# Turned weight blocks moved by sixteen transfers instead of ScalarE copies, with a new order of the last pair and a split last store

## The reference

```python
proj = h @ w_in[i]                      # token-mixer | memory query | gate columns
...
scores = jnp.einsum('bqhmd,bkhmd->bhmqk', q_blk, k) * scale
scores = jnp.where(causal, scores, NEG_BIG)
probs = jax.nn.softmax(scores, axis=-1)
weights = probs[:, :, 0] - lam * probs[:, :, 1]
out = jnp.einsum('bhqk,bkhe->bqhe', weights.astype(v.dtype), v)   # then RMSNorm per head
...
branch = jnp.concatenate([tok_out, cross_out], axis=-1) * jax.nn.silu(gate)
y = branch @ w_out[i]
x = x + _rms_norm(y, post_norm[i])
```

## Time and profile before

| | us |
|---|---|
| median of 3 runs (lowest to highest) | 956.06 (955.55 to 956.22) |
| the profiled execution | 956.12 |
| its span, first to last instruction | 954.3 |
| TensorE busy | 939.1 (98%) |
| VectorE busy | 632.1 (66%) |
| ScalarE busy | 504.3 (53%) |
| GpSimd busy | 1.2 |
| ScalarE's block copies, line 988, 96 in all | 34.6 |
| mean granted TensorE clock | 0.994 |

### The profile page before, as it was taken

How to read it: one execution, slowest core, us unless ns; L and a number is a source line. 1 busy time by engine, 2 the same in 40 slices (tenths; PEclk the granted TensorE clock), 3 DMA queues, 4 the chain that set the end, 5 groups by cost and what they waited for, 6 DMA issues and landing times.

```text
span 954.3 us, 12693 instructions
## 1 busy us (share of the span) xinstructions
PE 939.1 (98%) x4784; PEld 795.1 (83%) x4784; DVE 632.1 (66%) x826; ACT 504.3 (53%) x801; POOL 1.2 (0%) x9
## 2 busy tenths in 40 slices
PE   9999999999999999999999999999999999979996
PEld 7888888888888888888888888888888888868885
DVE  5878765754665475555685567466788888876555
ACT  6767633444434434444465456437577576574442
POOL 0000000000000000000000000000000000000000
PEclk9999999999999999999999999999999999989998
DMA  9757467667766666676566645664764764744552
GB/s 333 241 162 242 150 195 210 194 195 220 209 200 187 191 197 219 221 242 240 167 226 199 194 139 194 182 213 134 220 198 141 213 197 134 241 138 155 195 198 88
DMA packets 123870, 186.35 MB, mean 195 GB/s; under 512 B 6765, under 2 KB 66477, under 8 KB 123306
## 3 DMA queue, kind: packets, MB, share of 16 engines
q1 hardware_dynamic: 122138, 178.80, 60.2%
q10 hardware_dynamic: 1680, 6.85, 2.0%
HBM read 178.82 MB, written 2.10 MB: 190 GB/s over the span
## 4 chain that ended last, share of the span: by engine, by line
PE 96%; DVE 1%; DMA 1%; issue 1%; ACT 1%; SPq 0%; POOL 0%; DVEq 0%; POOLq 0%; ACTq 0%
PE psum L410 22%; PE psum L471 19%; PE psum L472 19%; PE psum L473 19%; PE psum L411 11%; PE psum L663 1%; DMA stage_area<-in_mem_dram 1%; PE psum L490 1%; PE psum L534 0%; DVE lo_ring L1040 0%; PE psum L511 0%; PE psum L652 0%; PE psum L644 0%; PE psum L643 0%; PE psum L642 0%
## 5 line engine op out<-in xcount | busy, mean ns | idle before, releaser
L1040 DVE TENSOR_TENSOR lo_ring<-raw_ring,hi_ring 128x1024 fp32r<-128x1024 f32 x318 | 386.0, 1222 | 261.7 <-ACT hi_ring L718 261.3
L718 ACT ACTIVATE hi_ring<-raw_ring 128x1024 fp32r<-128x1024 f32 x318 | 335.6, 1062 | 374.6 <-PE psum L473 275.3
L410 PE MATMUL psum<-hT_split,hi_ring 128*128 128x512 f32 x832 | 292.7, 397 | 0.0
L411 PE MATMUL psum<-hT_split,lo_ring 128*128 128x256 f32 x832 | 232.1, 279 | 0.0
L410 PEld LDWEIGHTS psum<-hT_split,hi_ring 128*128 128x128 f32 x832 | 156.1, 188 | 37.9 <-issue 2.0
L471 PE MATMUL psum<-hi_ring,hT_split 128*128 128x512 f32 x480 | 187.1, 390 | 0.0
L472 PE MATMUL psum<-lo_ring,hT_split 128*128 128x512 f32 x480 | 186.8, 389 | 0.0
L473 PE MATMUL psum<-hi_ring,hT_split 128*128 128x512 f32 x480 | 186.8, 389 | 0.0
L411 PEld LDWEIGHTS psum<-hT_split,lo_ring 128*128 128x128 f32 x832 | 156.8, 188 | 0.1
L473 PEld LDWEIGHTS psum<-hi_ring,hT_split 128*128 128x128 f32 x480 | 90.1, 188 | 18.8
L471 PEld LDWEIGHTS psum<-hi_ring,hT_split 128*128 128x128 f32 x480 | 90.1, 188 | 18.5
(11 more groups left out here) (225 smaller groups left out, 742.3 us busy)
## 6 DMA issues: line engine op xcount, KB each, us to landing
raw_ring<-in_w_in_dram SPq DMA_DIRECT2D x224, 512.0 KB, 3.8
raw_ring<-in_w_out_dram SPq DMA_DIRECT2D x64, 512.0 KB, 4.0
raw_ring<-in_w_kv_mem_dram SPq DMA_DIRECT2D x30, 512.0 KB, 4.1
layer_area<-layer_area SPq DMA_DIRECT2D x48, 64.0 KB, 3.5
x_residual<-in_conv_w_dram ACTq DMA_DIRECT2D x3, 768.0 KB, 6.0
stage_area<-in_mem_dram SPq DMA_DIRECT2D x8, 256.0 KB, 6.5
x_residual<-in_x_dram SPq DMA_DIRECT2D x2, 1024.0 KB, 8.6
layer_area<-in_post_norm_dram ACTq DMA_DIRECT2D x2, 1024.0 KB, 5.9
```

What stands on the lines that cost most here:

```text
L410: mm(o, hi[:, k, P * c:P * (c + 1)], X[:, kt, :], start=kt == 0, stop=False)
L411: last = mm(o[:, SEQ:], lo[:, k, P * c:P * (c + 1)], X[:, kt, 0:SEQ], start=False, stop=kt == KT - 1)
L718: run(whi[:, slot, :], raw[:, slot, :], ACT.Copy).then_inc(hi_ready, 1)
L1040: V_.tensor_tensor(wlo[:, slot, :], raw[:, slot, :], whi[:, slot, :].bitcast(f32), SUB)\
```

## The change

1. **Layout of the weights.** `prob` is now ordered map, head, key. VectorE turns each head by a transpose of its own, and writes each block with a stride, so that a block row of 192 words (32 queries, 2 heads, 3 key blocks) lies together.
2. **Sixteen transfers.** `move_weights` issues sixteen transfers of 32 rows x 192 words from ScalarE's queue, all in step 1 of the keys group. `diff_values` waits for all sixteen (256 on its semaphore) and reads the weights with a stride of six words.
3. **Last pair.** `softmax_max` of pair 5 goes one step earlier on VectorE. On TensorE the turn of pair 4 and the values of pair 5 both stand ahead of unit 2, and the turn of pair 5 ahead of unit 6. VectorE's `out_take` of pair 5 stands at step 4.
4. **Last store.** The first piece of the second row half leaves VectorE and SP: ScalarE scales it, GpSimd adds the residual, ScalarE issues its store. VectorE's last refinement step signals a semaphore of its own, `last_rstd_known`, in place of the running step count.

```diff
-STORES = [(0, 0, 1024), (0, 1024, 2048)] + [(1, ACOLS * g, ACOLS * (g + 1)) for g in range(4)]
+STORES = [(0, 0, 1024), (0, 1024, 2048)] + [(1, ACOLS * g, ACOLS * (g + 1)) for g in range(1, 4)]
...
-    prob = L1[:, 3072:4608].rearrange("p (h m k) -> p h m k", h=2, m=2)
-    probT = L1[:, 4608:5376].rearrange("p (h k) -> p h k", h=2)
-    prob_blocks = prob[:, :, 1, :]
+    prob = L1[:, 3072:4608].rearrange("p (m h k) -> p h m k", h=2, m=2)
+    probT = L1[:, 4608:5376].rearrange("p (a c) -> p a c", a=4)
+    prob_blocks = L1[:, 3840:4608]
...
+        pool.wait_ge(first_scaled, 1)
+        nc.gpsimd.tensor_tensor(xres[:, 1, 0:ACOLS], y_all[:, 1, 0:ACOLS], xres[:, 1, 0:ACOLS], ALU.add)\
+          .then_inc(first_added, 1)
...
         def diff_values(p):
-            pe.wait_ge(wt_ready, p * 16 + 16)
+            pe.wait_ge(wt_ready, p * 256 + 256)
+            weights = probT.rearrange("p a (r h k) -> p h k (a r)", h=2, k=3)
...
-                mm(o[:, 0:P], probT[:, h, 0:P], v[0], start=True, stop=True)
+                mm(o[:, 0:P], weights[:, h, 0], v[0], start=True, stop=True)
...
+        def last_values():
+            diff_out_turn(PAIRS - 2, PAIRS * 8)
+            diff_values(PAIRS - 1)
...
-                      at={0: lambda: diff_out_turn(PAIRS - 2, PAIRS * 8), 1: lambda: diff_values(PAIRS - 1),
-                          5: lambda: diff_out_turn(PAIRS - 1)} if g == 0 else {},
+                      at={2: last_values, 6: lambda: diff_out_turn(PAIRS - 1)} if g == 0 else {},
...
-        def move_weights(p, first, last):
-            act.wait_ge(blocks_turned, p + 1)
-            for a, b in QUADRANTS[first:last]:
-                to = probT.rearrange("p h (k a r) -> p h k a r", k=3, a=4)[32 * b:32 * b + 32, :, :, a, :]
-                block = prob_blocks.rearrange("p h (k b r) -> p h k b r", k=3, b=4)[32 * a:32 * a + 32, :, :, b, :]
-                run(to, block, ACT.Copy).then_inc(wt_ready, 1)
+        def move_weights(p):
+            act.wait_ge(blocks_turned, p * 2 + 2)
+            for a, b in QUADRANTS:
+                act.dma_start(probT[32 * b:32 * b + 32, a, :], prob_blocks[32 * a:32 * a + 32, 192 * b:192 * (b + 1)])\
+                   .then_inc(wt_ready, 16)
...
+        act.wait_ge(rstd_known, 2)
+        run(y_all[:, 1, 0:ACOLS], y_all[:, 1, 0:ACOLS], ACT.Copy, scale=y_rstd[:, 1:2]).then_inc(first_scaled, 1)
+        act.wait_ge(first_added, 1)
+        act.dma_start(out[0].rearrange("(p t) d -> p t d", p=P)[:, 1, 0:ACOLS], xres[:, 1, 0:ACOLS])\
+           .then_inc(out_stored, 16)
...
-            V_.transpose(prob_blocks, prob[:, :, 0, :]).then_inc(blocks_turned, 1)
+            for h in range(2):
+                blocks = prob_blocks.rearrange("p (b r h k) -> p h k b r", b=4, h=2, k=3)[:, h]
+                V_.transpose(blocks, prob[:, h, 0, :].rearrange("p (k b r) -> p k b r", k=3, b=4))\
+                  .then_inc(blocks_turned, 1)
...
-                     at={1: lambda: softmax_max(st, PAIRS - 1), 2: lambda: softmax_weights(st, PAIRS - 1, 1)})
+                     at={0: lambda: softmax_max(st, PAIRS - 1), 2: lambda: softmax_weights(st, PAIRS - 1, 1)})
...
-                          5: lambda: out_take(st, PAIRS - 1, 1)}
+                          4: lambda: out_take(st, PAIRS - 1, 1)}
...
-            op(V_.scalar_tensor_tensor(y, about, 1.5, y, ADD, MULT))
+            V_.scalar_tensor_tensor(y, about, 1.5, y, ADD, MULT).then_inc(rstd_known, 1)
+            dve.wait_ge(rstd_known, t + 1)
```

More of the change, by code:

```diff
@@ L219, in build @@
     gpost_loaded, out_stored = sem("gpost_loaded"), sem("out_stored")
+    rstd_known, first_scaled, first_added = sem("last_rstd_known"), sem("first_columns_scaled"), sem("first_columns_added")
     qrot_loaded, krot_loaded = sem("qrot_loaded"), sem("krot_loaded")
@@ L368, in _ @@
             sp.dma_start(out_v[:, t, lo_col:hi_col], xres[:, t, lo_col:hi_col]).then_inc(out_stored, 16)
-        sp.wait_ge(out_stored, 16 * len(STORES))
+        sp.wait_ge(out_stored, 16 * (len(STORES) + 1))
     @block.gpsimd
@@ L641, in diff_values @@
                 v = [V[:, t, bass.ds(p * (2 * P) + P * h, P)] for t in range(TT)]
-                mm(o[:, 0:P], probT[:, h, 0:P], v[0], start=True, stop=True)
-                mm(o[:, P:], probT[:, h, P:2 * P], v[0], start=True, stop=False)
-                last = mm(o[:, P:], probT[:, h, 2 * P:], v[1], start=False, stop=True)
+                mm(o[:, 0:P], weights[:, h, 0], v[0], start=True, stop=True)
+                mm(o[:, P:], weights[:, h, 1], v[0], start=True, stop=False)
+                last = mm(o[:, P:], weights[:, h, 2], v[1], start=False, stop=True)
             last.then_inc(pv_done, 1)
@@ L1010, in pair @@
             column_group(G + 1, u + B_UNITS, 1 - s,
-                         at={} if first else {1: lambda: move_weights(p - 1, 0, 8), 2: lambda: move_weights(p - 1, 8, 16)})
+                         at={} if first else {1: lambda: move_weights(p - 1)})
             column_group(G + 2, u + 2 * B_UNITS, s, at={} if first else {1: lambda: take_values(p - 1)})
@@ L1022, in _ @@
         column_group(G_XG1 + 1, U_XG1 + B_UNITS, (G_XG1 + 1) % 2,
-                     at={1: lambda: move_weights(PAIRS - 1, 0, 8), 2: lambda: move_weights(PAIRS - 1, 8, 16)})
+                     at={1: lambda: move_weights(PAIRS - 1)})
         tanh_of(G_XG1 + 1, val1, tanh1)
```

## The result

| | before | after |
|---|---|---|
| median of 4 runs each on one chip, us | 955.8 | 982.9 (981.3 to 984.4) |
| ratio to before, with its 95% interval | | 1.028 [1.026, 1.031] |
| span of the profiled execution, us | 954.3 | 979.5 |
| mean granted clock | 0.994 | 0.989 |

The changed kernel is 27 us slower. Forecast were 961.7 us, with a range that ended at 977.0.

A forecast was written before the change was run, and what follows sets the result against it. TensorE, busy 98% of the span, was taken as the bound nearly everywhere. Transfers +5.5, strided loads +2.1, last pair's order -1.5 and last store -0.5 summed to +5.6 us on a 956.06 median: 961.7 us, range 950.5 to 977.

The forecast's parts named there:

- The transfers in the inner pairs: Pairs 0 to 4: sixteen issues on ScalarE make TensorE wait 1.1 us for weights in each pair, +5.5 us.
- a granted clock below 0.9 between 650 and 840 us: Sign named in advance that, if seen anywhere in that stretch, would show the prediction wrong.
- They add nothing more: Inner pairs: ScalarE's casts queued behind the issues are ready before the delayed products are through, so no further cost.
- The strided loads: diff_values reading weights at a 24 B stride: 0.35 us per pair over six pairs, +2.1 us, bounds 0 and +7.6.
- The last pair and the order: Start of output stage: TensorE's 5.06 us wait moves to 4.1 us before unit 1; -1.5 us taken from -1.0 to -3.2.
- The sentence on the block: Last pair: with ScalarE's block gone altogether, the reordering would gain the whole -7.9 us.
- The last store: End of kernel: one of VectorE's four updates moves to ScalarE and GpSimd, -0.5 us, bounds -0.7 and +0.5.
- Cheap issues: Rival, 25%: ScalarE issues a transfer in 0.47 us, so the loop costs nothing and the tail gains 5.6; 952.1 us.
- The shared generator: Rival, 4%: SP's and ScalarE's queues share what makes descriptors, 3.5 us more per pair, +17.5, 979 us.
- half-pace loads: Rival, 8%: strided weight loads in diff_values run at half pace, +7.6 in place of 2.1; 967.2 us.
- half clock: Rival, 10%: each wait in the loop takes the clock down, 2.87 us lost five times, +14; 975.7 us.
- the likeliest: Whole kernel: the case as summed, +5.6 us, 961.7 us, by itself 957 to 967; chance 45%.

The follow-up runs named there:

- e2: The changed kernel with ScalarE's sixteen copies, in two runs of eight, in place of the transfers, new layout kept: 959.2 us.
- e1: The changed kernel with the old contiguous layout back under the transfers, each written in 192 pieces of 32 numbers: 975.7 us.
- e6: The changed kernel with TensorE's products and ScalarE's taking of their result one unit later in the inner pairs: 979.3 us.
- e14: e7 with only TensorE's weight loads of the values reading every sixth number (output meaningless, only time used): 956.6 us.
- e3: The kernel before with only the changed kernel's order of the last pairs and last store; ScalarE still copies: 949.0 us.
- e7: The kernel before with the last pairs' new order alone; ScalarE's copies and the old last store stay: 948.5 us.
- e8: The kernel before with the new last store alone: 956.1 us, ratio 1.000.
- e9: The changed kernel with the same sixteen transfers issued by GpSimd in place of ScalarE: 970.1 us.
- e11: e9 with each transfer in 192 pieces into the old contiguous layout, and the old last store: 968.5 us.

## Why the prediction was wrong

**What bounds the kernel** was right: TensorE is the path nearly everywhere, and every microsecond of the result is a wait of TensorE, its clock behind one, or a slower load.

**The transfers in the inner pairs** are the step that failed most: +5.5 predicted, +14.4 in the five periods (207.7 of after against 193.3 of e2). The mechanism is right, sixteen issues on one engine, then the landing. Its terms, all from the mark of the scores, pair 3, predicted and measured: start 13.4 and 13.8; first to last issue 9.1 and about 9.6 (10.15 less one issue); last landing 2.8 and 3.5; TensorE asks at 24.2 and 24.9. That makes 1.1 and 2.0 (2.07 by the profile, 2.0 to 2.5 over the five pairs). Each term was a little low, and in a difference of two sums of 24 us the small errors were the size of the answer. The median landing (2.8 chosen, 3.1 measured) was also the wrong number: the slowest of sixteen counts, and it may be any of them.

The remaining 3.4 us of the 14.4 are **clock**. Pairs 0 and 1 lie 4.6 and 3.3 over e2, pairs 2 to 4 about 2.2. "Mine are a quarter of it, so I hold it unlikely" rested on a wait of 1.1; at 2.0 to 2.5 us the clock fell in two of five pairs, and in e1, at 2.2 to 3.3 us, behind four of five. So that rival was partly true, and its sign, a granted clock below 0.9 between 650 and 840 us, was there (0.50 at 671 to 675).

**"They add nothing more"**, said of the casts behind the issues, is true of the changed kernel and misleading as a reading: e6 showed 1.7 us of delay hidden beside the other, so that taking the first away gave 3.5 us where 14.4 were expected.

**The strided loads** were mis-sized: +2.1 predicted, +8.1 measured (e14). I took VectorE's 1.26 at 12 B as the nearest row and half pace as a rival at 8%. Half pace is what it is: 0.445 us from one product to the next in place of 0.22. My upper bound, 7.6, was nearly the value. The Trainium skill (SBUF — State Buffer, "Door 1: The DMA port swizzle") pointed to a cost larger than that row's, and the trace agrees: products at a 24-byte stride take 2.1 times as long (2.59 in e2 for 1.26). The price of the **transposes**, which write the same stride, was in the sum only as a later start; what is left for it by subtraction (e2, e3, e7 and e14) is 2.0 us.

**The last pair and the order**: -1.5 predicted. The steps came out one by one, a wait of 4.5 us for 4.1, the clock down behind it, VectorE not yet in the way. But 2.6 us for the products (886.41 to 889.00) stood where I had 1.6, and from the end of the last group to unit 2 it took 889.00 - 873.48 = 15.5 us where before took 15.0. That the transfers are what eats the gain, e2 shows: with copies its tail is 120.0 us, 6.3 under before, and with transfers 127.1. The sentence on the block was wrong in another way. -7.9 was tied to "ScalarE's block gone altogether"; e7 has the block and gets -7.3, because a cast stands in the middle of it.

**The last store**: -0.5 predicted; e8 finds none (1.000 [0.999, 1.001]), e3 is 0.5 us slower than e7, within their scatter. The case that I kept as the upper bound, that addition and updates exclude each other, is what the rows show: 1.73 us of GpSimd for at most 1.2 expected, and 3.08 for three updates of 0.69, one of which takes 1.75.

**The rivals.** Cheap issues (25%) is out: 0.612 median. The shared generator, as priced, is out: beside pair 3's block SP issued its four swaps in 2.55 us (2.41 before, rows 7), and ScalarE its sixteen in 10.15, not 3.5 us later. Only beside pair 0's block did the swaps take 3.26. SP's timeline there:

```profile
790.06 2.55 SPq L347 DMA_DIRECT2D layer_area<-layer_area  x4
```

Of the other two, half-pace loads were wholly true and half clock partly, and I had laid out each alone. Added to the likeliest, the one as I priced it and the other as it came, they give 961.7 + 5.5 + 3.4 = 971. The rest up to 982.9 is mainly the wait in the pairs (11.0 for 5.5), the transposes (2.0) and tail and store (+0.8 for -2.0); 1.6 lie between the profiled execution and the median. The range failed because it took one rival at a time.

## What to carry to other kernels

Work taken off an engine that is not the bound gained nothing here, and a row of sixteen small transfers on that engine's queue blocked it for longer (10.2 us) than the copies did (two runs of 3.1 with a cast between). Before replacing copies by transfers, count issues times spacing plus the slowest landing, and look for every instruction queued behind them. And when terms come out as the difference of large sums, or several rivals can be true together, the range must hold their sum.

## What the runs showed of the hardware

- Weight loads of TensorE at a stride of 24 B take 317 ns at the median in e9 against 192 contiguous (e11). The products with them follow each other at 0.445 us at a granted clock of 1.00, and at 0.50 too (672.65 to 673.10 in pair 0 of the changed kernel). Contiguous ones follow at 0.22 us at 1.00, and at 0.43 at the lower level (e1, pair 2).
- A transfer on chip of 24 KB costs its issuer 0.61 us on ScalarE and 0.50 on GpSimd. In six times as many pieces 0.63 and 0.57.
- GpSimd's addition of two 128x512 tiles takes 1.73 us, and one of VectorE's updates beside it is held up (1.75 us for 0.75), so that three take 3.08 us.
- A wait of 2.5 and one of 2.15 us in a busy stretch were followed by a lower clock in pairs 0 and 1 of the changed kernel, waits of 2.0 to 2.1 in pairs 2 to 4 were not. In e1 the clock fell behind waits of 3.3, 2.5, 2.2 and 2.2 us and stayed up behind one of 2.3, so the length of the wait alone does not tell.
